# Logits of the cached sequences against A's pages, x's raw transposes and half of the B cache row copies in other places of a decoder layer

## The reference, cut to what matters

```
h  = RMSNorm_pre(x)
[qA kA vA fA zA | qB kB vB zB | gA gB] = h @ w_in
A: 8 heads x 64, logits += C[t] - C[s];  B: 3 groups x 4 heads x 64, dilations 1, 4, 16
u_A = (o_A * silu(zA)) @ w_br_a ; u_B = (o_B * silu(zB)) @ w_br_b
x  = x + RMSNorm_post((sigmoid(gA) * u_A + sigmoid(gB) * u_B) @ w_out)
x  = x + sigmoid(x @ w_ple_gate) * RMSNorm_ple(p[i] @ w_ple)

def fox_sample(q, k_new, v_new, logf_new, kv_pool, logf_pool, page_table):   # A, cached sequences
    past = kv_pool[page_table]                 # 4 pages of 128 positions for each sequence
    ...
    s = jnp.einsum("nqhd,nkhd->nhqk", q, k).astype(jnp.float32) * ATTN_SCALE
    ...
    return jnp.einsum("nhqk,nkhd->nqhd", p, v).astype(q.dtype)

def dilated_sample(q, k_new, v_new, bufs, rel_bias):                         # B, cached sequences
    ...
        ext = jnp.concatenate([buf, jnp.stack([k_new[:, :, g], v_new[:, :, g]], axis=2)], axis=1)
        ...
        new_bufs.append(ext[:, T:])            # the window buffer, shifted by one row, is an output
```

## Time and profile before

| what | us |
|---|---|
| median of 3 runs | 682.23 (680.82 to 684.08) |
| the profiled execution | 685.89 |
| its span in the trace | 684.0 |

### The profile page before, as it was taken

How to read it: one execution, slowest core, us unless ns; L and a number is a source line. 1 busy time by engine, 2 the same in 40 slices (tenths; PEclk the granted TensorE clock), 3 DMA queues, 4 the chain that set the end, 5 groups by cost and what they waited for, 6 DMA issues and landing times.

```text
span 684.0 us, 12648 instructions
## 1 busy us (share of the span) xinstructions
PE 632.6 (92%) x4810; PEld 589.1 (86%) x4810; DVE 368.6 (54%) x881; ACT 242.2 (35%) x559; POOL 139.0 (20%) x159
## 2 busy tenths in 40 slices
PE   3999999999999999999899789899699979999893
PEld 3988989999898999999799788877469979999893
DVE  3774554454555444533666776333127755588742
ACT  7824343443434333243322113332103366344210
POOL 5032101010100400000656777011102332000000
PEclk9999999999999999999999989999958999999997
DMA  8339836261621762412189996767711166212121
GB/s 252 93 107 355 278 97 209 71 197 50 193 70 32 249 215 63 121 43 84 35 286 284 288 305 165 206 184 212 224 55 55 34 171 179 62 42 62 37 57 33
DMA packets 105674, 98.42 MB, mean 144 GB/s; under 512 B 6484, under 2 KB 93832, under 8 KB 105329
## 3 DMA queue, kind: packets, MB, share of 16 engines
q1 hardware_dynamic: 102000, 71.64, 36.6%
q0 software_dynamic: 3568, 25.99, 10.6%
q10 hardware_dynamic: 48, 0.01, 0.0%
HBM read 90.31 MB, written 26.14 MB: 170 GB/s over the span
## 4 chain that ended last, share of the span: by engine, by line
PE 70%; DVE 7%; SPq 6%; DMA 5%; issue 5%; ACT 4%; POOL 3%; POOLq 0%; DVEq 0%; ACTq 0%
PE pj L818 42%; PE tr L810 5%; PE tr L818 5%; PE pv L943 3%; PE sc L910 3%; DMA kv_b<-in_cache_b_kv_dram 3%; PE sc L918 2%; SPq L495 2%; SPq L497 2%; PE sc L818 1%; POOL prod L674 1%; ACT w_hi L1144 1%; POOL prod L678 1%; SPq L501 1%; PE sc L915 1%
## 5 line engine op out<-in xcount | busy, mean ns | idle before, releaser
L818 PE MATMUL pj<-h_hi,w_hi 128*128 128x256 f32 (+1 forms) x960 | 287.0, 299 | 11.2 <-ACT gsig L1174 11.2
L818 PE MATMUL pj<-h_lo,w_hi 128*128 128x256 f32 (+1 forms) x960 | 276.2, 288 | 0.0
L818 PE MATMUL pj<-h_hi,w_lo 128*128 128x256 f32 (+1 forms) x960 | 275.6, 287 | 0.0
L818 PEld LDWEIGHTS pj<-h_hi,w_hi 128*128 128x128 f32 x960 | 186.3, 194 | 25.6 <-issue 24.0
L818 PEld LDWEIGHTS pj<-h_lo,w_hi 128*128 128x128 f32 x960 | 186.4, 194 | 0.0
L818 PEld LDWEIGHTS pj<-h_hi,w_lo 128*128 128x128 f32 x960 | 185.9, 194 | 0.0
L1398 DVE TENSOR_TENSOR w_lo<-w_raw,w_hi 128x1024 fp32r<-128x1024 f32 (+2 forms) x84 | 96.5, 1152 | 44.7 <-ACT w_hi L1144 44.2
L1144 ACT ACTIVATE w_hi<-w_raw 128x1024 fp32r<-128x1024 f32 (+2 forms) x84 | 81.7, 973 | 97.6 <-PE pj L818 40.3
L1405 DVE COPY probT<-tr 128x256 f32<-128x256 f32 (+3 forms) x56 | 27.4, 489 | 52.6 <-PE tr L810 52.6
L674 POOL TENSOR_TENSOR prod<-kv_a,qbc 128x512 f32<-128x512 f32 x24 | 33.7, 1432 | 20.3 <-DMA kv_b<-in_cache_b_kv_dram 15.3
L818 PE MATMUL tr<-h_hi,w_hi 128*128 128x256 f32 (+1 forms) x128 | 36.9, 288 | 0.5 <-issue 0.5
(11 more groups left out here) (368 smaller groups left out, 994.7 us busy)
## 6 DMA issues: line engine op xcount, KB each, us to landing
w_raw<-in_w_in_dram SPq DMA_DIRECT2D x52, 512.0 KB, 4.7
kv_a<-in_cache_a_kv_dram SPq DMA_DIRECT2D x64, 256.0 KB, 3.5
out_dram<-in_cache_b_kv_dram POOLq DMA_DIRECT2D x16, 1022.0 KB, 9.9
qbc<-q_dram SPq DMA_DIRECT2D x8, 640.0 KB, 5.4
kv_b<-in_cache_b_kv_dram SPq DMA_DIRECT2D x32, 128.0 KB, 3.1
w_raw<-in_w_out_dram SPq DMA_DIRECT2D x8, 512.0 KB, 4.1
w_raw<-in_w_ple_gate_dram SPq DMA_DIRECT2D x8, 512.0 KB, 4.1
x_in<-in_x_prompt_dram SPq DMA_DIRECT2D x4, 512.0 KB, 5.5
```

The costliest lines, as they stand in the source:

```text
L818: ins = nc.tensor.matmul(out, w[:, k0, :], x[:, c_x, lo:hi], start=first and i == 0, stop=last and i == 2)
```

## The change

- **A's logits of the cached sequences** are made in steps i = 1 to 8 of rounds 6 to 9, two sequences in a round: in round 4 at i = 9 a new turn puts the four A heads' q of the cached tokens together, Pool writes it to DRAM; SP (`keys_a`) loads q (256 KB) and four pages for a sequence between the weight loads; Pool multiplies all four pages (32 products of 128x512, three buffers), DVE reduces one product in each step. `prod_v` is gone. ACT's first gate evacuation waits until all 32 reduces are over, because buffers share memory.
- **The gate stage** keeps the B logits: q is 384 KB, slices have buffers of their own, 24 products of 128x256, eight buffers; DVE reduces two sequences in each of t = 1 to 4. SP's loads of the value pages of sequences 0 and 1 come ahead of the three small DMAs. The softmax moves from t = 10 to t = 6, the probabilities from t = 12 to t = 8, and the values stand one sequence behind each of t = 9 to 16.
- **The raw transposes of x** (8 turns, and the one of the cached tokens) go to i = 11 of round 0, i = 9 and 11 of rounds 1 to 3, and i = 11 of round 4.
- **The row copies**: two of `b1` in front of each of rounds 1 to 4, none in rounds 5 to 8; the eight of `b2` are issued by Pool in the branch stage, one for each m, ahead of its wait for `h_hi` of tile m.

```diff
-PRODS = 4
+PRODS, RPRODS = 8, 3
-RAW = (ROUNDS - 3, ROUNDS - 2)
+R_QA, R_LOGITS = ROUNDS_A, ROUNDS_A + 2
+RAW_AT = {0: {11: 0}, 1: {9: 1, 11: 2}, 2: {9: 3, 11: 4}, 3: {9: 5, 11: 6}, 4: {11: 7}}
+T_ROWS, T_PROBS, T_VALUES = 6, 8, 9
...
+            def keys_a(s):
+                if s == 0:
+                    sp.wait_ge(S["s_qad"], 16)
+                    sp.wait_ge(s_pt, 16)
+                if s >= 2:
+                    sp.wait_ge(S["s_prod"], PAGES * (s - 1))
+                sp.dma_start(qbc_r[s % 2][:, :], qa_dram[s:s + 1, :].to_broadcast([P, AW])).then_inc(S[f"s_qb{s % 2}"], 16)
+                pages(s, 0, kv_r)
+            for r in range(ROUNDS_A + 1, ROUNDS + 1):
+                for j in range(3):
+                    load(3 * r + j)
+                    if r > R_LOGITS and j < 2:
+                        keys_a(2 * (r - 1 - R_LOGITS) + j)
...
             for s in range(DEC):
                 sample_queries(s)
                 if s:
-                    sample_rows(s, 0)
+                    slices(s, 0, kv_k)
+                if s % 2:
+                    load(n)
+                    n += 1
+            for s in range(2):
+                pages(s, 1, kv_a)
                 load(n)
                 n += 1
-            for k in range(3):
-                load(n + k)
-            sp.wait_ge(S["s_prod"], 6 * DEC)
-            sp.wait_ge(S["s_prodv"], DEC)
+            sp.wait_ge(S["s_prod"], (PAGES + BG) * DEC)
+            for s in range(2):
+                slices(s, 1, kv_b)
             sp.wait_ge(S["s_slfd"], 48)
...
             for s in range(2, DEC):
+                load(n)
+                n += 1
                 sp.wait_ge(S["s_samp"], s - 1)
-                sample_rows(s, 1)
+                pages(s, 1, kv_a)
+                slices(s, 1, kv_b)
...
+                if r <= ROUNDS_A:
+                    copy_rows(1, 2 * r - 2, 2 * r - 1)
+                    copy_rows(1, 2 * r - 1, 2 * r)
...
+                if r >= R_LOGITS and r < ROUNDS:
+                    for s in (2 * (r - R_LOGITS), 2 * (r - R_LOGITS) + 1):
+                        pool.wait_ge(S[f"s_qb{s % 2}"], 16 * (s // 2 + 1))
+                        pool.wait_ge(S[f"s_kp{s % 2}"], 64 * (s // 2 + 1))
+                        for p in range(PAGES):
+                            k = PAGES * s + p
+                            if k >= RPRODS:
+                                pool.wait_ge(S["s_red"], k - RPRODS + 1)
+                            nc.gpsimd.tensor_tensor(prod_r[k % RPRODS][:, :], kv_r[s % 2][:, p, :], qbc_r[s % 2][:, :], ALU.mult).then_inc(S["s_prod"], 1)
...
-            with pool.Fori(0, DC) as m:
+            for m in range(DC):
+                copy_rows(2, m, m + 1)
                 pool.wait_ge(S["s_mh"], m + 1)
...
+                    if i in RAW_AT.get(r, ()):
+                        c = RAW_AT[r][i]
                         turn([(P, b * P, x_in[:, b, c * P:(c + 1) * P]) for b in range(NB)])
+                    if r == R_QA and i == 9:
+                        turn([(DEC, k * P, samp[:, 3 * k, :]) for k in range(ROUNDS_A)])
...
-                if t == 10:
+                if t == T_ROWS:
                     sample_rows_t(pe, turn)
-                if 13 <= t < 17:
-                    sample_values(pe, t - 13)
-                if t >= 17:
-                    sample_values(pe, 2 * t - 30)
-                    sample_values(pe, 2 * t - 29)
+                if T_VALUES <= t < T_VALUES + DEC:
+                    sample_values(pe, t - T_VALUES)
...
+                    if i in RAW_AT.get(r, ()):
+                        out_of_turn((xT[:, RAW_AT[r][i], 0:SEQ], lambda b: b[:, :]))
+                    if r >= R_LOGITS and r < ROUNDS and 1 <= i < 9:
+                        logits_a(PAGES * 2 * (r - R_LOGITS) + i - 1)
```

More of the change, by code:

```diff
@@ L236, in build @@
         cursor[0] = after_g
+        qa_tok = sb("qa_tok", [DEC, AW], at=at_g)
+        kv_r = [sb(f"kv_r{i}", [P, PAGES, AW], at=at_g + 4 * 3 * T if i == 0 else None) for i in range(2)]
+        qbc_r = [sb(f"qbc_r{i}", [P, AW]) for i in range(2)]
+        prod_r = [sb(f"prod_r{i}", [P, AW]) for i in range(RPRODS)]
+        assert cursor[0] <= after_g
+        cursor[0] = after_g
         at_2 = cursor[0]
@@ L280, in build @@
         self_p = sb("self_p", [DEC, ROUNDS, P], at=at_3 + 3 * ROUNDS * P * 4 + PAGES * AW * 4)
-        qbc = [sb(f"qbc{i}", [P, AW + BQ], at=at_2 + i * 4 * (AW + BQ)) for i in range(2)]
-        prod = [sb(f"prod{i}", [P, AW]) for i in range(PRODS)]
-        prod_v = sb("prod_v", [P, AW])
+        qbc = [sb(f"qbc{i}", [P, BQ], at=at_2 + i * 4 * BQ) for i in range(2)]
+        kv_k = [sb(f"kv_k{i}", [P, BG, BO]) for i in range(2)]
+        prod = [sb(f"prod{i}", [P, BO]) for i in range(PRODS)]
         assert cursor[0] <= at_3
@@ L477, in _, with pages, slices @@
                     load(3 * r + 5)
[L478 to L482, removed]
+            def pages(s, kv, bufs):
+                for p in range(PAGES):
+                    page = sp.value_load(pt[0:1, PAGES * s + p:PAGES * s + p + 1], min_val=0, max_val=POOL_PAGES - 1)
+                    src = A["cache_a_kv"][0, bass.ds(page, 1), :, kv, :, :].rearrange("o t h d -> (o t) (h d)")
+                    sp.dma_start(bufs[s % 2][:, p, :], src).then_inc(S[f"s_kp{s % 2}"], 16)
+            def slices(s, kv, bufs):
+                for g in range(BG):
+                    n, step = SLOTS[g], DIL[g]
+                    src = caches[g][0, s, 0:n * step:step, kv, :, :].rearrange("t h d -> t (h d)")
+                    sp.dma_start(bufs[s % 2][0:n, g, :], src).then_inc(S[f"s_bk{s % 2}"], 16)
+            def keys_a(s):
[11 more added lines that the diff above has]
+                        keys_a(2 * (r - 1 - R_LOGITS) + j)
+            for n in range(TILE_G + 3, TILE_G + 7):
                 load(n)
@@ L506, in _ @@
             sp.wait_ge(S["s_comb"], 1)
-            sp.wait_ge(s_pt, 16)
-            sample_rows(0, 0)
+            slices(0, 0, kv_k)
             sp.wait_ge(S["s_qd"], 16)
@@ L525, in _ @@
             sp.dma_start(sm[0:DEC * BH, 1:1 + BG], selfb_dram.rearrange("s (h g) -> (s h) g", g=BG)).then_inc(S["s_selfr"], 16)
[L526 to L531, removed]
+            for k in range(T_VALUES - 4):
+                load(n)
+                n += 1
             for s in range(2, DEC):
+                load(n)
+                n += 1
                 sp.wait_ge(S["s_samp"], s - 1)
-                sample_rows(s, 1)
+                pages(s, 1, kv_a)
+                slices(s, 1, kv_b)
+            for k in range(3):
                 load(n)
```

136 lines of the change are left out of this document (56 added, 80 removed).

## The result

| what | before | after |
|---|---|---|
| median of 20 runs each, us | 683.01 (678.91 to 689.90) | 679.29 (673.87 to 688.37) |
| ratio, 95% interval | | 0.9947 (0.9922 to 0.9973) |
| the profiled execution, us | 685.89 | 676.29 |
| its span, us | 684.0 | 674.5 |

The kernel is faster by 0.5%, where 2.4% was forecast (666, 653 to 678). The two traces differ by 9.5 us, the medians by 3.7: single executions of one kernel lie 8 to 9 us apart even without the longest of each, 689.90 and 688.37.

The account below looks back on a forecast made before the run. PE was taken to bound most of the kernel, with late weights costing the gate stage some 16 us. Terms -22.8 + 0.5 + 4.5 + 0.4 + 1.5 = -15.9 took 685.9 to 670.0, less 3.7 to the median: 666, range 653 to 678.

Parts of the forecast that it names:

- a pair takes about 7 us: Gate stage: two sequences in flight take 1.7 + 3.1 + 2.13 us for issue, landing and Pool's products.
- no weight waits over 2 us: Gate stage: a sign of being right, ACT never waiting more than 2 us for raw weights.
- Rival (2): Gate stage: the chain to the softmax is longer, t = 8 starts 4 to 9 us later, 670 to 675; chance 0.15.
- rival (5): Gate stage loses the same to weight loads behind waits for products, only the end is won: 681; chance 0.14.
- the two waits of silu: Gate stage, t = 17 and 18: without values covering silu's way through ACT and DVE, two waits of 1.4 us.
- -6.4 for idles: End of the gate stage: PE idles of 1.47 and 4.93 us go, as pages are asked for two tiles ahead.
- -6.9 for the clock: End of the gate stage: 9.9 us given back from work at 1.2 GHz, less 3 kept for returning dips.
- the splits `w_lo`: Rounds 6 to 9: three splits per round up to 1.1 us later beside Pool's products; 0.5 us taken, bounds 0 to 5.
- (3): Rounds 6 to 9: a rival in which DVE waits for Pool's products, given 8 us; chance 0.07.
- The raw turns: Round boundaries: turns at i = 11 idle PE 0.95 us five times, shorter in round 0; +4.5 us, bounds 0 and 6.
- The 1.5 taken: Branch stage: eight row copies make weight loads land later, mostly covered; +1.5 us, bounds 0 and 6.
- Rival (1): Branch stage and first p and output tiles: row copies starve weight loads, costing 18 to 35 us, 684 to 700; chance 0.07.

Follow-up runs that it names:

- loads: Changed kernel with two more gate-stage weight loads issued by SP ahead of the first key slices: 677.96 us, 0.9917 of before.
- small: Changed kernel with the softmax's three small DMAs issued ahead of the first value pages, once sequence 6's products are over: 681.85 us, 0.9991 of before.
- both: Changed kernel with two more weight loads ahead of the first key slices and the softmax's small DMAs ahead of the value pages: 672.60 us, 0.9855 of before.
- ends: Changed kernel with the values, and SP's order of pages, slices and weight loads, back where they stood before: 687.90 us, 1.0086 of before.
- port: Changed kernel with Pool's products in rounds 7 to 9 begun only after DVE has both row maxima: 674.53 us, 0.9898 of before.
- turns: Changed kernel with the raw transposes of step i = 11 moved to i = 10: 676.46 us, 0.9928 of before.
- copies: Changed kernel with row copies back to one of b1 and one of b2 ahead of rounds 1 to 8, none in the branch stage: 678.96 us, 0.9937 of before.
- v11: Changed kernel with the eight sequences' values behind t = 11 to 18 in place of 9 to 16: 675.86 us, 0.9907 of before.

## Why the prediction was wrong, step by step

It forecast 666.3; 679.3 came, 13 us more.

**The gate stage up to t = 8.** The bound was read rightly: SP's order, with the weight loads behind the waits for Pool's products. The step that failed is the size of this chain, "a pair takes about 7 us" and what SP issues behind it. By the weight loads the pairs take 8.3 to 9.0, and q and slices of sequence 7 are out 25.1 us after the end of t = 0 and not 22.1. From there to the end of the last small DMA's issue SP takes 16.3 and not 12.5; six slices alone took 3.65 where 2 x 1.40 were counted. Against it, from there to DVE's softmax it took 2.1 and not 4.4. So t = 8 began 48.6 after t = 0 and not 44.1: 4.5 us. The forecast also promised no weight waits over 2 us; at one load per pair of sequences that couldn't be, by its own 7 us against 5.76. Rival (2) named this, with 4 to 9 us, and rival (5) the weight loads. loads, small and both show that both chains were late: mending both is worth 6.7 to 7.9 by the medians.

**From t = 8 to the end of m = 0.** 97.8 us were worked out, 97.4 came in the trace (98.1 in the second). This step was right on the side of after, and term by term nearly so: the two waits of silu are 2.0 for 2.8, and the clock, 0.96 in these 97.4 us, costs some 3.9 where 3 were kept. The step that failed is on the side of before: the gain was counted against one execution whose slow stretch was 23.9 us. The sum -6.4 for idles, -6.9 for the clock, +2.8 for silu makes 10.5 for the values' new places; ends puts them back for 7.4 to 8.6: 2 to 3 us too many. In the second trace of before the same way, from t = 12 (429.56) to the end of m = 0 (512.05), took 82.5 and not the 85.3 that the sum starts from: 2.8 less. Taking 3.7 off at the end, to come from that execution to the median, moved its total and not this term.

**A's logits in the rounds.** That a DVE instruction gets longer beside Pool's products (1.78 for 0.67) was the right thing to look for; the place was wrong. The forecast looked at the splits `w_lo`, 1.1 us each, with slack, and took 0.5. The port run measures 4.8 to 6.0. `w_lo` grew by 0.9 and 0.3 in round 7 alone, within its slack; the cost lay on `nm_b` in rounds 8 and 9, which is small, has ACT and PE behind it at once, and was held till the third of three products ended (3.16 us for 0.17), not for part of one. No run shows the 8 us given to (3), DVE waiting for Pool's products in rounds 6 to 9: these waits are 3.4 us in the first trace of after, in five waits of up to 2.2, and 4.2 in the second, in five of up to 3.0. Only 2.3 of the 4.8 to 6.0 are idles; dips of the clock that went with them are the likely rest, not shown apart.

**The raw turns.** Right: 0.95 five times, less in round 0, was forecast, 4.5; 0.52 + 4 x 0.77 = 3.6 were in the trace, and turns takes back 2.8 to 4.1. The copy waits for the split as worked out; the idle is 0.2 shorter each.

**The row copies.** The 1.5 taken is neither borne out nor refuted. The stretch behind m = 0 is 169.57 in both traces of after, where before has 168.91 and 166.85 and copies 168.96; but in port and v11, with the copies in it, it is 167.8 and 167.7. Rival (1) did not come: from 505 to 560 the weight loads of the output projection landed after 4.6 us and those of the p job after 3.9, where copies has 4.4 and 2.2. So the copies were felt, but not by the tens of us that (1) needs.

**The account.** From trace to trace the forecast was 6.4 us off: a span of 684.0 - 15.9 = 668.1 was due, and 674.5 came. The windows have it: 3.2 in the rounds (8.6 for 5.4), 4.1 between the ends of t = 0 and m = 0 (18.7 for 22.8), 0.8 less behind. Of the 8.6 in the rounds, 3.6 are the raw turns, 2.3 the idles behind `nm_b`, 0.9 the later start; if q's turn costs the 0.4 that was forecast, 1.4 are not located. The other 6.7 of the 13 lie between executions: 3.7 that the forecast took off to come from the traced execution of before to its median, though it had counted its gain in that execution's long slow stretch, and 3.0 by which the traced execution of after lies below its own median. Why one execution of a kernel takes a few us more than another stays open.

## What to carry to other kernels

When a stage is moved from one bound to another, work out the new period of every chain in it (here q and slices, weight loads, small DMAs) and set it against the period of the engine to be fed; where two chains end within a few us, mending one gives little or nothing (1.3 to 2.6 us and none here, 6.7 to 7.9 for both). Before moving work to Pool, look not only for the longest DVE instructions beside it but also for the shortest on whose result another engine stands (here `nm_b`, 0.17 us alone and 3.16 beside the products). And a gain that rests on the clock should be counted from more than one execution, since a slow stretch behind the same idle was 13.7 us in one trace and 23.9 in others.

## What the runs showed of the hardware

A DVE scaling of 128x4 numbers, 0.17 us alone (port), took 3.16 us when it met Pool multiplying (after, rounds 8 and 9), and ended with the third product in a row, not the first. So it was held over more than one instruction of Pool; whether a longer row of products would hold it longer, no run shows. Row copies of 1 MB, one per tile of 4.5 us, beside weight loads in a stage whose DMAs had been busy 0.18 of the time, left the time unchanged within what can be told (679.29 and 680.52 with them, 678.96 in copies). In the rounds, beside two copies (copies), a weight load landed after 13.1 us where it took 5.6 without them (after), and at 49 us, beside a pile of them, one after 24.6.
